# Two-layer diffusion trunk on one core: experts combined in token order, a last norm along the free axis, one-hot turns moved behind the first weight product

## The chip, the cores and the metric

One Trainium2 chip; the kernel runs on one of its cores. The time is device microseconds of one launch, the median of the runs; lower is better. The instruction streams of the core's engines are written out by hand and meet only at semaphores: TensorE (PE, with its weight loads PEld), VectorE (DVE), ScalarE (ACT), GpSimd (POOL) and SyncE (SP), which here issues the weight loads.

## What is computed

256 tokens of width 1024, with 256 context tokens, go through two layers. Only the end of the second layer concerns the change: a mixture of 8 experts, of which each token takes two, and the gated residual with its RMS norm.

```python
def moe_swiglu(h, router_w, w1, w3, w2):
    logits = (h @ router_w).astype(jnp.float32)
    top_val, top_idx = lax.top_k(logits, TOP_K)          # TOP_K = 2
    gates = jax.nn.softmax(top_val, axis=-1)
    dense_gate = jnp.sum(jax.nn.one_hot(top_idx, N_EXPERTS) * gates[..., None], axis=-2)
    out = jnp.zeros_like(h)
    for e in range(N_EXPERTS):                           # 8, inner width 3584
        out = out + dense_gate[..., e:e + 1] * swiglu(h, w1[e], w3[e], w2[e])
    return out
```

The layer ends with `x + gate * rmsnorm(moe_swiglu(...), g)`, where gate (from the conditioning) and g are vectors of width 1024. All arithmetic is held to fp32 accuracy: a matrix is split into a high and a low fp32r part, and a product is three products of those parts.

## The kernel before

**Weights.** SyncE loads all weights in units of 1 MB (128 x 2048 fp32) into a ring of six buffers, `raw_weights` (`RAW`), in one fixed order. An expert has 42 units (`NU`), numbered u0 to u41: for each of seven column blocks j two units of w1 (item "a"), two of w3 ("b") and two of w2 ("d"), in the order a0 b0, then a(j) b(j) d(j-1), and d6 last. ScalarE copies a unit to its high part (L1207), VectorE subtracts for the low part (L1523); there are three pairs of buffers for the parts (two are `split_high`/`split_low`, the third lies in `h_high`/`h_low`), so ScalarE waits until TensorE has used the pair. A raw buffer is free once its low part is made. The loads of the first expert take the buffers that the last earlier units leave: u0 the one of the last modulation weights, u1 the one of the router weights, which the router's last product (L1747) frees, and SyncE takes u2 to u5 behind u1.

**Start of the experts.** After the norm, TensorE multiplies by the router weights and transposes the normed tokens into token-major form (L1747, L1753). ScalarE and VectorE split these into `HTH` and `HTL` (L1169, L1431), VectorE finds the top two, the gates (`GATE`, tokens on partitions) and each token's slot in each expert, TensorE counting the positions (L1761 to L1765). VectorE makes one-hot matrices token by slot, `expert_onehot` (`MP`, L1467). `dispatch(0, r)` (L1798) gathers the first expert's tokens with them, in two halves of 16 products. Then TensorE turns all one-hots (L1785, ScalarE evacuates to `expert_onehot_t`, `MPT`, L1198), and multiplies them by the gates to get a gate for each slot (`slot_gates`, L1777). VectorE copies these (L1483), clears two banks and starts on the low parts of u0 and u1.

**One expert.** Up products write banks 0 to 3, down products accumulate in banks 4 and 5, slot by feature. The output of expert e-1 is handled inside expert e: `gated` (VectorE) scales banks 4 and 5 by the slot gate into `residual` (L1494), ScalarE makes the high part `ye_high` (L1190), VectorE the low part `ye_low` (L1501); `combine` (TensorE, L1870 and L1871, between a0 and b0) multiplies them by the turned one-hots, 16 products of 256 columns, which gives feature by token; `gather` (VectorE, L1510) adds four banks to `y` (`YACC`). For the first expert this handles a zero output, so there are nine combines. `dispatch(e + 1, r)` stands between d5 and d6 of expert e, on both sides of the last turn of the hidden state (L1840); it runs for the last expert too, with an empty one-hot.

**The end.** `YACC` is feature-major, so the last norm (n7) sums squares across partitions: ScalarE squares eight tiles (L351), TensorE sums (L365), ScalarE takes the root (L359), VectorE the reciprocal (L398), TensorE spreads it over partitions (L378), VectorE scales and adds to the residual (L449, L461), TensorE transposes the result (L1915), ScalarE evacuates (L1233) and SyncE stores two halves of 512 KB (L969). A branch for more than 128 tokens in an expert stands behind the experts; every engine reads its flag there.

## Time and profile before

| | |
|---|---|
| median of 3 runs | 2055.4 us (2053.35 to 2057.25) |
| the profiled execution, own time | 2057.55 us |
| its span, first to last instruction | 2055.7 us |
| busy: PE, DVE, ACT | 1928.8 (94%), 1296.7 (63%), 1088.1 (53%) us |
| granted TensorE clock, mean | 0.96 |
| HBM read | 471.25 MB, 230 GB/s over the span |

Times in the profile count from the span's first instruction. A timeline row gives start, duration and, in square brackets, the idle time of the engine before it and what ended it. Durations of matmuls are modelled and overlap; the difference between two starts is the pace. The granted clock is 1.00 at 2.4 GHz and 0.50 at 1.2 GHz.

### The profile page before, as it was taken

What the parts mean: (1) busy time and instruction counts of PE and PEld (TensorE: products, weight loads), DVE (VectorE), ACT (ScalarE), POOL (GpSimd) and SP (SyncE); (2) the same over time, 40 slices, a digit from 0 to 9 for tenths busy, and PEclk for the clock granted to TensorE, in tenths of its full rate; (3) what the DMA queues carried; (4) which work ended last, traced back from release to release, by engine and by line L of the source; (5) the groups of instructions that cost most, each with busy time, mean ns of one, the idle gap of its engine ahead of it and who ended that gap; (6) DMA issues with size and microseconds to landing.
All of it is one profiled execution on the core that took longest, in us unless ns stands there. A gap on an engine that the chain in (4) does not pass through costs nothing.

```text
span 2055.7 us, 24073 instructions
## 1 busy us (share of the span) xinstructions
PE 1928.8 (94%) x9978; PEld 1539.3 (75%) x9978; DVE 1296.7 (63%) x1252; ACT 1088.1 (53%) x1109; POOL 28.5 (1%) x44
## 2 busy tenths in 40 slices
PE   4998798999999989888899999999999999999996
PEld 2876476888878777457788787887888878888784
DVE  2344725323233462453788888888888888888885
ACT  3423435222232363354476676767767677676773
POOL 0000000000000000310000000000000000000000
PEclk9998899999999999897799999999999999999997
DMA  9453164533222270331699998999989999899990
GB/s 320 144 164 123 33 193 145 167 98 103 102 83 85 95 226 29 86 97 59 237 377 345 331 363 316 372 337 332 377 312 368 337 334 369 318 364 344 345 367 27
DMA packets 263942, 473.97 MB, mean 231 GB/s; under 512 B 17112, under 2 KB 116368, under 8 KB 263824
## 3 DMA queue, kind: packets, MB, share of 16 engines
q1 hardware_dynamic: 262928, 469.31, 65.2%
q0 software_dynamic: 896, 3.02, 0.5%
q8 instruction: 82, 1.34, 0.3%
q14 instruction: 36, 0.29, 0.0%
HBM read 471.25 MB, written 1.05 MB: 230 GB/s over the span
## 4 chain that ended last, share of the span: by engine, by line
PE 82%; DVE 9%; ACT 4%; DMA 2%; issue 2%; SPq 1%; POOL 0%; DVEq 0%; ACTq 0%
PE bank L508 24%; PE bank L510 23%; PE bank L509 23%; DVE split_low L1523 3%; PE bank L717 2%; PE bank L1798 2%; PE bank L571 2%; PE bank L1840 1%; DMA raw_weights<-in_w_mod 1%; PE bank L691 1%; DVE y L1510 1%; DVE h_low L1523 1%; PE bank L706 1%; SPq L907 1%; PE bank L365 1%
## 5 line engine op out<-in xcount | busy, mean ns | idle before, releaser
L1523 DVE TENSOR_TENSOR split_low<-raw_weights,split_high 128x2048 fp32r<-128x2048 f32 x224 | 512.5, 2288 | 53.3 <-ACT split_high L1207 51.5
L1207 ACT ACTIVATE split_high<-raw_weights 128x2048 fp32r<-128x2048 f32 x224 | 429.9, 1920 | 158.9 <-PE bank L510 158.9
L508 PE MATMUL bank<-h_high,split_high 128*128 128x512 f32 (+1 forms) x848 | 326.2, 385 | 21.7 <-DVE h_low L422 9.9
L492 DVE TENSOR_TENSOR split_low<-raw_weights,split_high 128x1024 fp32r<-128x1024 f32 x118 | 143.6, 1224 | 307.3 <-ACT split_high L487 307.3
L509 PE MATMUL bank<-h_low,split_high 128*128 128x512 f32 (+1 forms) x848 | 323.5, 381 | 0.0
L510 PE MATMUL bank<-h_high,split_low 128*128 128x512 f32 (+1 forms) x848 | 323.2, 381 | 0.0
L1523 DVE TENSOR_TENSOR h_low<-raw_weights,h_high 128x2048 fp32r<-128x2048 f32 x112 | 256.7, 2292 | 71.8 <-ACT h_high L1207 71.8
L508 PE MATMUL bank<-split_high,xe_high 128*128 128x512 f32 x672 | 270.7, 403 | 11.5 <-DVE split_low L1523 11.5
L509 PE MATMUL bank<-split_low,xe_high 128*128 128x512 f32 x672 | 265.9, 396 | 0.0
L510 PE MATMUL bank<-split_high,xe_low 128*128 128x512 f32 x672 | 265.9, 396 | 0.0
L1207 ACT ACTIVATE h_high<-raw_weights 128x2048 fp32r<-128x2048 f32 x112 | 214.9, 1919 | 53.2 <-PE bank L510 53.2
L487 ACT ACTIVATE split_high<-raw_weights 128x1024 fp32r<-128x1024 f32 x118 | 123.7, 1055 | 193.5 <-PE bank L510 189.3
L508 PEld LDWEIGHTS bank<-h_high,split_high 128*128 128x128 f32 x848 | 164.0, 193 | 54.5 <-issue 17.4
L510 PEld LDWEIGHTS bank<-h_high,split_low 128*128 128x128 f32 x848 | 163.7, 193 | 29.8
L509 PEld LDWEIGHTS bank<-h_low,split_high 128*128 128x128 f32 x848 | 164.1, 193 | 28.9
L508 PEld LDWEIGHTS bank<-split_high,xe_high 128*128 128x128 f32 x672 | 126.7, 189 | 42.5 <-issue 14.8
L510 PEld LDWEIGHTS bank<-split_high,xe_low 128*128 128x128 f32 x672 | 126.6, 188 | 30.3
L509 PEld LDWEIGHTS bank<-split_low,xe_high 128*128 128x128 f32 x672 | 126.9, 189 | 28.0
L508 PE MATMUL bank<-h_high,xe_high 128*128 128x512 f32 x224 | 89.1, 398 | 1.9 <-DVE h_low L1523 1.9
L508 PE MATMUL bank<-split_high,gt_high 128*128 128x512 f32 x224 | 89.1, 398 | 0.0
L508 PE MATMUL bank<-h_high,gt_high 128*128 128x512 f32 x224 | 88.5, 395 | 0.0
L509 PE MATMUL bank<-h_low,gt_high 128*128 128x512 f32 x224 | 88.5, 395 | 0.0
(246 smaller groups left out, 2630.4 us busy)
## 6 DMA issues: line engine op xcount, KB each, us to landing
raw_weights<-in_moe_w SPq DMA_DIRECT2D x336, 1024.0 KB, 6.7
raw_weights<-in_w_mod SPq DMA_DIRECT2D x48, 1024.0 KB, 6.0
raw_weights<-in_ffn_w SPq DMA_DIRECT2D x33, 1024.0 KB, 5.3
raw_weights<-in_ev_w_in SPq DMA_DIRECT2D x10, 1024.0 KB, 11.9
raw_weights<-in_od_w_in SPq DMA_DIRECT2D x8, 1024.0 KB, 7.1
raw_weights<-in_ev_w_out SPq DMA_DIRECT2D x4, 1024.0 KB, 8.9
raw_weights<-in_od_w_out SPq DMA_DIRECT2D x4, 1024.0 KB, 9.8
overlay<-in_rpb SPq DMA_DIRECT2D x32, 64.0 KB, 2.3
```

The costliest lines, as they stand in the source:

```text
L365: last = pe.matmul(n["sums"](j, t), ones[:, 0:32], n["sq"][:, t % 2, P * j:P * j + P], start=(t == 0 or n["single"]), stop=(t == n["nt"] - ...
L487: act.activation(half_of(s, j, SPH[:, s % NSPLIT, :]), half_of(s, j, raw_of(r)), ACT.Copy)\
L492: dve.tensor_tensor(half_of(s, j, SPL[:, s % NSPLIT, :]), half_of(s, j, raw_of(split_at[s])), half_of(s, j, SPH[:, s % NSPLIT, :]).bitcast ...
L508: pe.matmul(ps, wh, xh, start=first, stop=False)
L509: pe.matmul(ps, wh, xl, start=False, stop=False)
L510: return pe.matmul(ps, wl, xh, start=False, stop=last)
L571: last = pe.matmul(PS[bank][32 * j:32 * j + 32, 256 * (i % 2):256 * (i % 2) + 256], SC[:, 4 * h + j, :], wt[:, 4 * h + j, :], start=(h == ...
L691: last = pe.matmul(PS[2 * (i % 2) + m][:, :P * u["nk"]], u["q"][m], u["k"][m], start=True, stop=True)
L717: last = pe.matmul(pair_out(units, p)[0], u["v"][kt], PT[p % 2][:, kt, :], start=(kt == 0), stop=(kt == u["nk"] - 1))
L1207: act.activation(esplit(u)[0], RAW[:, u % NRAW, :], ACT.Copy).then_inc(S("e_high"), 1)
L1523: dve.tensor_tensor(lo, RAW[:, u % NRAW, :], hi.bitcast(F32), ALU.subtract)\
L1798: last = pe.matmul(PS[XBANK[r]][:, P * f:P * f + P], half[:, t, k:k + P], rhs, start=(n == 0), stop=(n == 3))
```

## The change

1. **Combine in token order.** `combine` takes the turned one-hots as the stationary operand and the high and low parts of the ungated output as the moving one: 8 products of 512 columns, token by feature. The gate is a scalar for each partition there, so `gather` becomes one multiply-add per bank with `GATE` as the scalar (for the first expert a plain multiplication). `gated`, `slot_gates`, the slot gates, the clearing of banks and of `YACC`, the ninth combine and the ninth dispatch go. ScalarE makes `ye_high` straight from banks 4 and 5.
2. **Last norm along the free axis.** `YACC` is token-major, so ScalarE squares four tiles with an accumulated row sum, and no cross-partition sum or spread is left. The product of conditioning gate and norm gain is needed as rows: VectorE builds eight diagonal tiles ahead of the router's result (`GDIAG`), TensorE sums them with a matrix of ones (two fp32 products of 512 columns) and ScalarE copies the result to `GROW`. TensorE transposes the residual without waiting for the norm; VectorE does the final multiply-add straight into the store buffer, and SyncE stores four pieces of 256 KB.
3. **Order at the start.** The high parts of u0 and u1 are made by ScalarE ahead of the copies of the token-major tokens; the low part of u0 by VectorE ahead of the router's result and that of u1 behind the first one-hot. The other one-hots come behind `xe_low`. TensorE turns the one-hots behind a0 instead of ahead of it, into banks 6, 7, 2 and 3. The table for Silu is loaded ahead of the experts, the one for Sqrt ahead of `moe_done`, VectorE's first instruction behind the branch.

The diff, cut to its core (counters of semaphores that only change their factor are left out):

```diff
+            for i in range(4):
+                t, c = i // 2, i % 2
+                sp.wait_ge(S("out_ready"), i + 1)
+                sp.dma_start(out[0, P * t:P * t + P, 512 * c:512 * c + 512], OUTT[:, i, :]).then_inc(S("stored"), 16)
+            sp.wait_ge(S("stored"), 64)
...
+            act.wait_ge(*unit_used(of["odo"][-1]))
+            for u in range(2):
+                act.wait_ge(S(f"eraw{u}"), 16)
+                act.activation(esplit(u)[0], RAW[:, u, :], ACT.Copy).then_inc(S("e_high"), 1)
...
+            for c in range(2):
+                act.wait_ge(S("grow_full"), c + 1)
+                act.activation(GROW[c], PS[6 + c][:, :].rearrange("p (a n) -> p a n", a=2), ACT.Copy)\
+                   .then_inc(S("grow"), 1)
+            act_table(act, ACT.Silu, 52)
...
+                    act.wait_ge(S("e_slots"), g0 + (e + 1) * NU + NSP_E)
                     for c in range(2):
-                        act.wait_ge(S("yg"), e * 2 + (2 * (NE + 1) * b + c + 1))
-                        act.activation(YEH[:, 512 * c:512 * c + 512], YG[:, 2 * c:2 * c + 2, :], ACT.Copy)\
+                        act.activation(YEH[:, 512 * c:512 * c + 512], PS[4 + c][:, :], ACT.Copy)\
                            .then_inc(S("ye_high"), 1)
...
+                            if b == 0 and e == 0 and u < 2:
+                                continue
...
-            act_squares(act, N["n7"])
-            act_root(act, N["n7"])
+            act_table(act, ACT.Sqrt, 53)
+            act.wait_ge(S("moe_done"), 1)
             for i in range(4):
-                act.wait_ge(S("out_full"), i + 1)
-                act.activation(OUTT[:, i // 2, 512 * (i % 2):512 * (i % 2) + 512], PS[i][:, :], ACT.Copy)\
-                   .then_inc(S("out_ready"), 1)
+                act.activation(SQUARED[i], YACC[i], ACT.Square, accum_out=SM[:, 12 + i:13 + i])\
+                   .then_inc(S("out_squares"), 1)
+            act.wait_ge(S("out_sums"), 1)
+            act.activation(SM[:, 18:20], SM[:, 16:18], ACT.Sqrt, bias=SM[:, 0:1], scale=1.0 / D).then_inc(S("out_root"), 1)
...
+            for k in range(KT):
+                last = dve.tensor_scalar(GDIAG[:, k // 2, k % 2, :], ident, VEC[:, 1, 3, k, 1:2], None, ALU.mult)
+            last.then_inc(S("grow_diag"), 1)
...
+            dve.wait_ge(S("e_high"), 1)
+            low_of(0)
...
+                onehot(0).then_inc(S("onehot_first"), 1)
                 if b == 0:
-
-                    dve.memset(GSL[:, 0:1], 0.0)
-                    dve.memset(MPT[:, 0, :].bitcast(F32), 0.0)
+                    dve.wait_ge(S("e_high"), 2)
+                    low_of(1)
                 xe_low(0, 0)
                 xe_low(0, 1)
-                if b == 0:
-                    link(dve, dve.memset(YACC, 0.0))
-                dve.wait_ge(S("gslot_full"), b + 1)
-                dve.tensor_copy(GSL[:, 1:NE + 1], PS[5][:, 32:40]).then_inc(S("gslot"), 1)
-                dve.wait_ge(S("gslot"), b + 1)
-                if b == 0:
+                for e in range(1, NE):
+                    last = onehot(e)
+                last.then_inc(S("onehot"), 1)
+
+                def ye_low(e):
+
                     for c in range(2):
-                        dve.memset(PS[4 + c][:, :], 0.0).then_inc(S("y_clear"), 1)
-                    dve.wait_ge(S("y_clear"), 2)
-
-                def gated(e):
-
-                    dve.wait_ge(S("e_slots"), e * NU + (g0 + NSP_E))
-                    for c in range(2):
-                        dve.tensor_scalar(YG[:, 2 * c:2 * c + 2, :],
-                                          PS[4 + c][:, :].rearrange("p (a n) -> p a n", a=2),
-                                          GSL[:, e:e + 1] if isinstance(e, int) else GSL[:, bass.ds(e, 1)], None,
-                                          ALU.mult).then_inc(S("yg"), 1)
-                    for c in range(2):
...
                     for r in range(4):
-                        dve.wait_ge(S("comb_full"), e * 4 + (4 * (NE + 1) * b + r + 1))
-                        acc = YACC[:, 2 * r:2 * r + 2, :]
...
+                        t, c = r % 2, r // 2
+                        dve.wait_ge(S("comb_full"), 4 * (NE * b + e) + r + 1)
...
+                        else:
+                            dve.scalar_tensor_tensor(acc, part, GATE[:, t, e:e + 1], acc, ALU.mult, ALU.add)\
+                               .then_inc(S("comb_done"), 1)
...
             dve.tensor_scalar(SM[:, 61:62], SM[:, 0:1], 1.0, None, ALU.mult).then_inc(S("moe_done"), 1)
-            dve_rstd(dve, N["n7"])
-            dve_residual(dve, N["n7"], 1, 1, 256)
+            dve.wait_ge(S("moe_done"), 1)
+            for i in range(4):
+                dve.tensor_tensor(OUTT[:, i, :].rearrange("p (a n) -> p a n", a=2), YACC[i], GROW[i % 2], ALU.mult)\
+                   .then_inc(S("out_scaled"), 1)
+            dve.wait_ge(S("out_squares"), 4)
+            sums = SM[:, 12:16].rearrange("p (t c) -> p t c", t=2)
+            dve.tensor_tensor(SM[:, 16:18], sums[:, :, 0], sums[:, :, 1], ALU.add).then_inc(S("out_sums"), 1)
+            dve.wait_ge(S("out_root"), 1)
+            link(dve, dve.reciprocal(SM[:, 20:22], SM[:, 18:20]))
+            dve.wait_ge(S("out_scaled"), 4)
+            for i in range(4):
+                dve.wait_ge(S("out_full"), i + 1)
+                dve.scalar_tensor_tensor(OUTT[:, i, :], OUTT[:, i, :], SM[:, 20 + i // 2:21 + i // 2],
+                                         PS[(0, 1, 4, 5)[i]][:, :], ALU.mult, ALU.add).then_inc(S("out_ready"), 1)
...
+            pe.wait_ge(S("grow_diag"), 1)
+            for c in range(2):
+                pe.matmul(PS[6 + c][:, :], ones, X[:, 4 + 2 * c:6 + 2 * c, 0:256], start=True, stop=True)\
+                  .then_inc(S("grow_full"), 1)
...
-                pe.wait_ge(S("onehot"), b + 1)
-                turn_onehots()
-                slot_gates()
-                pe.wait_ge(S("mpt_done"), 4 * b + 4)
-                if b == 0:
-                    pe.wait_ge(S("y_clear"), 2)
-                pe.wait_ge(S("gslot"), b + 1)
...
+                        if i == 0:
+                            pe.wait_ge(S("xe_low"), 2 * (NE * b + e) + q + 1)
...
-                        for f in range(2):
-                            k = P * (2 * r + f)
-                            o = PS[CBANK[r]][:, 256 * f:256 * f + 256]
...
-                            pe.matmul(o, YEH[:, k:k + P], rhs, start=True, stop=False)
-                            last = pe.matmul(o, YEL[:, k:k + P], rhs, start=False, stop=True)
-                        last.then_inc(S("comb_full"), 1)
+                        t, c = r % 2, r // 2
+                        pe.wait_ge(S("ye_low"), 2 * (NE * b + e) + c + 1)
+                        turned, y = MPT[:, e, P * t:P * t + P], slice(512 * c, 512 * c + 512)
+                        pe.matmul(PS[CBANK[r]][:, :], turned, YEH[:, y], start=True, stop=False)
+                        pe.matmul(PS[CBANK[r]][:, :], turned, YEL[:, y], start=False, stop=True)\
+                          .then_inc(S("comb_full"), 1)
...
-                            if j == 1:
-
-                                pe.wait_ge(S("comb_done"), e * 4 + (4 * (NE + 1) * b + 4))
+                            if j == 1 and e == 0:
+                                pe.wait_ge(S("mpt_done"), 4 * b + 4)
+                            elif j == 1:
+                                pe.wait_ge(S("comb_done"), 4 * (NE * b + e))
                             up(e, i, "a", j).then_inc(S("e_slots"), 1)
-                            if j == 0:
-                                combine(e)
+                            if j == 0 and e == 0:
+                                pe.wait_ge(S("onehot"), b + 1)
+                                turn_onehots()
+                            elif j == 0:
+                                combine(e - 1)
...
-                                dispatch(e + 1, 0)
+                                if e + 1 < NE:
+                                    dispatch(e + 1, 0)
                                 turn(e, JE - 1)
-                                dispatch(e + 1, 1)
+                                if e + 1 < NE:
+                                    dispatch(e + 1, 1)
...
-            pe_sums(pe, N["n7"])
-            pe_spread(pe, N["n7"])
-
             for i in range(4):
-                pe.wait_ge(S("n7_res"), 4 * (i % 2) + 4)
                 for k in range(4):
                     src = X[:, 4 * (i % 2) + k, CTX + P * (i // 2):CTX + P * (i // 2) + P]
-                    last = pe.transpose(PS[i][:, P * k:P * k + P], src, ident)
```

ScalarE's order from the normed tokens to the first expert; names in brackets are semaphores, `eraw1` is the landing of u1, `xe_full` the dispatch. Before:

```order
L345 ACTIVATE small<-small 128x1
L1169 ACTIVATE h_high<-bank 128x512 [waits htok_full] x4
L1172 ACTIVATE overlay<-overlay 128x2 [waits top_diff]
L1178 ACTIVATE xe_high<-bank 128x512 [waits xe_full] x2
L1198 ACTIVATE expert_onehot_t<-bank 128x512 [waits pt_full] x4
L1207 ACTIVATE split_high<-raw_weights 128x2048 [waits e_slots,eraw0]
L1207 ACTIVATE split_high<-raw_weights 128x2048 [waits e_slots,eraw1]
```

The changed kernel:

```order
L345 ACTIVATE small<-small 128x1
L1169 ACTIVATE split_high<-raw_weights 128x2048 [waits eraw0,bank_full]
L1169 ACTIVATE split_high<-raw_weights 128x2048 [waits eraw1]
L1174 ACTIVATE h_high<-bank 128x512 [waits htok_full] x4
L1177 ACTIVATE overlay<-overlay 128x2 [waits top_diff]
L1180 ACTIVATE residual<-bank 128x2x256 [waits grow_full] x2
L345 ACT_TABLE_LOAD
L345 ACTIVATE small<-small 128x1
L1188 ACTIVATE xe_high<-bank 128x512 [waits xe_full] x2
```

The two splits of weights moved from behind the turned one-hots to ahead of the four token copies. VectorE's order at a change of expert, before:

```order
L1523 TENSOR_TENSOR split_low<-raw_weights,split_high 128x2048 [waits e_high] x2
L1494 TENSOR_SCALAR residual<-bank,overlay 128x2x256 [waits e_slots]
L1494 TENSOR_SCALAR residual<-bank,overlay 128x2x256
L1501 TENSOR_TENSOR ye_low<-residual,ye_high 128x512 [waits ye_high] x2
L1523 TENSOR_TENSOR h_low<-raw_weights,h_high 128x2048 [waits e_high]
L1523 TENSOR_TENSOR split_low<-raw_weights,split_high 128x2048 [waits e_high]
L1510 TENSOR_TENSOR y<-bank,y 128x2x256 [waits comb_full] x4
L1523 TENSOR_TENSOR split_low<-raw_weights,split_high 128x2048 [waits e_high]
```

The changed kernel:

```order
L1424 TENSOR_TENSOR split_low<-raw_weights,split_high 128x2048 [waits e_high] x2
L1516 TENSOR_TENSOR ye_low<-bank,ye_high 128x512 [waits ye_high] x2
L1424 TENSOR_TENSOR h_low<-raw_weights,h_high 128x2048 [waits e_high]
L1424 TENSOR_TENSOR split_low<-raw_weights,split_high 128x2048 [waits e_high]
L1529 SCALAR_TENSOR_TENSOR y<-bank,overlay,y 128x2x256 [waits comb_full] x4
L1424 TENSOR_TENSOR split_low<-raw_weights,split_high 128x2048 [waits e_high]
```

The two gatings (L1494) are gone and nothing took their place; the adds became multiply-adds.

## Rows read from the trace of the kernel before

**Rows 1.** The expert phase, 1020 to 2020 us, by windows: length; busy PE PEld DVE ACT POOL; clock, DMA share, GB/s.
```profile
1020.00:2020.00 1000.00, 990.90 (x4546) 806.70 (x4545) 862.40 (x514) 700.48 (x469) 0.00 (x0) 1.00 0.94 342
```

**Rows 2.** Waits of 1020 to 2026 us: waiter, releaser, us in total, times, longest.
```profile
PE bank L508 <- DVE split_low L1523: 7.2, 7, 1.0
```

**Rows 3.** TensorE's timeline at one change of expert: start, duration, engine, line, operation.
```profile
1266.05 0.28 PE L1871 MATMUL bank<-expert_onehot_t,ye_low 128*128 128x256 f32 x1
1266.86 0.50 PE L508 MATMUL bank<-h_high,xe_high 128*128 128x512 f32 x1 [0.53 <-DVE h_low L1523]
...
1272.31 0.40 PE L510 MATMUL bank<-split_high,xe_low 128*128 128x512 f32 x1
1273.75 0.47 PE L508 MATMUL bank<-split_high,xe_high 128*128 128x512 f32 x1 [1.04 <-DVE split_low L1523]
```

**Rows 4.** VectorE's timeline at the same change of expert.
```profile
1260.60 1.41 DVE L1494 TENSOR_SCALAR residual<-bank,overlay 128x512 f32<-128x512 f32 x2
1262.05 1.35 DVE L1501 TENSOR_TENSOR ye_low<-residual,ye_high 128x512 fp32r<-128x512 f32 x2
...
1268.93 2.48 DVE L1510 TENSOR_TENSOR y<-bank,y 128x512 f32<-128x512 f32 x4
```

**Rows 5.** ScalarE's timeline at the same change of expert.
```profile
1261.38 1.29 ACT L1190 ACTIVATE ye_high<-residual 128x512 fp32r<-128x512 f32 x2 [3.02 <-DVE residual L1494]
1262.58 1.90 ACT L1207 ACTIVATE h_high<-raw_weights 128x2048 fp32r<-128x2048 f32 x1
```

**Rows 6.** TensorE's timeline from the first dispatch to the first weight product.
```profile
981.73 0.47 PE L1798 MATMUL bank<-expert_onehot,h_high 128*128 128x128 f32 x1 [2.75 <-DVE expert_onehot L1467]
...
988.62 3.62 PE L1785 MATMUL bank<-ident_r,expert_onehot 128*128 128x128 f32 x16
...
1002.90 0.77 PE L508 MATMUL bank<-split_high,xe_high 128*128 128x512 f32 x1 [3.95 <-DVE split_low L1523]
```

**Rows 7.** VectorE's timeline ahead of the first dispatch.
```profile
974.55 0.24 DVE L1411 COPY overlay<-bank 128x8 f32<-128x8 f32 x2 [6.04 <-PE bank L1747]
...
976.54 2.47 DVE L1431 TENSOR_TENSOR h_low<-bank,h_high 128x512 fp32r<-128x512 f32 x4
...
981.20 3.21 DVE L1467 TENSOR_SCALAR expert_onehot<-constants,overlay 128x128 fp32r<-128x128 f32 x16
```

**Rows 8.** SyncE's only expert load between 974.0 and 974.8 us, and its landing.
```profile
L920 SPq DMA_DIRECT2D raw_weights<-in_moe_w x1: 368/368/368, 974.5 to 974.5; - x1
...
DMA to landing us min/median/max: 5.1/5.1/5.1
```

**Rows 9.** The first 3 us of the weight products, by windows.
```profile
1003.00:1006.00 3.00, 3.00 (x7) 2.35 (x8) 3.00 (x3) 0.35 (x1) 0.00 (x0) 0.50 0.62 190
```

**Rows 10.** The costliest groups of 812 to 817 us: count, busy us, mean ns.
```profile
L1685 PE MATMUL bank<-raw_weights,overlay 128*128 128x512 f32 x8 | 3.7, 604 | 0.0
```

**Rows 11.** Timelines of VectorE and TensorE around the last expert's last down product.
```profile
2015.39 2.29 DVE L1523 TENSOR_TENSOR h_low<-raw_weights,h_high 128x2048 fp32r<-128x2048 f32 x1 [0.51 <-ACT h_high L1207]
...
2019.91 0.48 PE L508 MATMUL bank<-split_high,gt_high 128*128 128x512 f32 x1
```

**Rows 12.** VectorE's timeline from the last expert's end.
```profile
2025.79 1.41 DVE L1494 TENSOR_SCALAR residual<-bank,overlay 128x512 f32<-128x512 f32 x2 [4.36 <-PE bank L510]
...
2028.76 2.48 DVE L1510 TENSOR_TENSOR y<-bank,y 128x512 f32<-128x512 f32 x4 [0.17 <-PE bank L1871]
2033.88 0.15 DVE L1552 TENSOR_SCALAR small<-small 128x1 f32<-128x1 f32 x1 [2.63 <-issue]
```

**Rows 13.** ScalarE's timeline of the last norm and the output.
```profile
2038.58 1.28 ACT L359 ACT_TABLE_LOAD   x1
2039.88 0.36 ACT L359 ACTIVATE overlay<-bank,small 64x128 f32<-64x128 f32 x1
...
2052.09 0.60 ACT L1233 ACTIVATE overlay<-bank 128x512 f32<-128x512 f32 x1 [0.26 <-PE bank L1915]
```

**Rows 14.** ScalarE reading a row sum out of its accumulator (attention, earlier in the run).
```profile
881.30 0.19 ACT L733 ACTIVATION_READ_ACCUMULATOR y<-y,small 128x1 f32 x1
```

117 lines of the change are left out of this document (55 added, 62 removed).

## The prediction

> **What bounds the kernel now.** I read the windows first, then the waits, then the timelines of the three places that the change touches. The windows say that the expert phase is TensorE's: 990.9 of 1000 us busy at the full clock, while the DMA engines are 0.94 busy and VectorE 862 us [rows 1]. Nothing spread over that phase on another engine is worth anything; what counts is what TensorE executes there and where it stands still. The waits name VectorE's low parts, one kind of them once per change of expert, 7 times [rows 2]. Then there is a serial stretch on each side of the phase: from the router to the first weight product at 1002.90 [rows 6], and from the last combine to the end at 2055.7 [rows 12, 13]. In both TensorE's clock is low, but the engines wait for one another, so single latencies count.
>
> **1. Changes of expert.** TensorE starts the first product of b0 at 1266.86 where the pace of the combine (0.12) would have it at 1266.17: 0.69 lost. It starts a1 at 1273.75, and the pace of a 512-column product (0.23) would have given 1272.54: 1.21 lost [rows 3]. Together 1.90 us, at 7 changes 13.3 us. Both times a low part came late. VectorE had just done two gatings (1.41), two subtractions (1.35) and, later, four adds (2.48) [rows 4] beside its 2.29 per unit [rows 11]; and ScalarE had idled 3.02 us for the gated values, which put its high part of u2 off to 1262.58 [rows 5].
> In the changed kernel ScalarE makes `ye_high` as soon as the last down product is over (about 1258.9 on this clock) instead of at 1261.38, so its high part of u2 comes 2.4 us earlier, at 1260.2 to 1262.1. VectorE then does `ye_low` 1260.6 to 1262.0, u2 to 1264.4, u3 to 1266.6, the four multiply-adds to 1269.0 and u4 to 1271.2 (paces 2.2 and 0.62 from the rows). TensorE's combine is 8 products at 0.233 = 1.87 against 16 at 0.12 = 1.9: nothing gained or lost. It wants u2 at 1266.2 (1.8 to spare) and u4 at 1271.8 (0.6 to spare). I take both stalls as gone: **-13.3**. From below: a multiply-add out of PSUM is in no row; if it costs 0.1 more than the add, u4 still makes it; if it costs twice the add (2.5 more per change), u4 is 1.9 late and the gain is only the first stall, 0.7 x 7 = 4.8. From above: TensorE's other idle time is small, so 13.3 is nearly the end of what is there.
>
> **2. Start.** Removed from TensorE's way are the turns (3.62) and the slot gates behind them, with what followed: VectorE's copy, two clears and the low part of u0, the end of which is the wait of 3.95 before the first weight product [rows 6]. Now that product may follow the first dispatch at once. Dispatch ran from 981.73 to 988.62, so 1002.90 would become 988.7, **-14.2** [rows 6]. The turns come back behind a0 in the place of the first, empty combine, 16 products of 128 columns (half of 3.62, 1.8, at the full clock) against 1.9, even.
> But the change puts a wait on this path. ScalarE now makes the high part of u1 ahead of its copies of the tokens, and u1's load is issued at 974.5, when the router's product has freed the buffer, and lands 5.1 later, at 979.6 [rows 8]. Queued behind it on ScalarE: four copies, the exponential of the gates, the `GROW` copies, a table load. A unit's high part takes 1.90 [rows 5], so the copies start at 981.5 and the first is done at 982.1. VectorE's four token low parts, which began at 976.54 [rows 7], can begin at 982.1: **5.6 later**, and everything behind them (gates, positions, first one-hot, dispatch) moves by as much. First dispatch 987.3, first weight product 994.2: **-8.7** net. One more half microsecond comes back at a1, since u4 and u5 are no longer behind an empty gather; **-9.2** in all.
> At no cost, with their cover: the eight diagonals (0.20 each as the one-hots of [rows 7], 1.6) and u0's low part (2.3) lie in VectorE's 6.04 us of waiting for the router [rows 7]: u0's high part is made by about 972.2, its low part by 974.5, when the wait ends; without that cover they cost up to 3.9. The two `GROW` products: eight fp32 instructions of 512 columns took 3.7 at the full clock [rows 10], a product shows as two, so four at half the clock are 3.5 us. TensorE was idle 2.75 us before the dispatch [rows 6] and gets 5.6 more. The `GROW` copies (1.2) and the table load (1.3) fit between the exponential and the end of the first half of the dispatch, 3.4 us behind its start. Low part of u1: 2.3 under the dispatch.
> The clock: the first 3 us of weight products ran at half speed [rows 9]; I leave that as it is. If it rises at once, 1.6 more is gained; if it takes twice as long, 1.6 is lost.
>
> **3. Last expert.** Without the ninth dispatch d6 waits only for the last hidden state's turn, high and low part. VectorE is at u41 from 2015.39 until 2017.7 [rows 11], then makes `gt_low` (0.7): d6 can start at 2018.4 instead of 2019.91, **-1.5**. The 3.5 us of products removed are thus not all gained: a wait for VectorE takes their place.
>
> **4. End.** VectorE gates from 2025.79, right behind the last product, ScalarE and VectorE split, and the gather ends at 2031.24 [rows 12]. Without gating the combine starts 0.7 earlier, the gather ends at 2030.6. Then 2.63 us of flag and branch, kept, so `moe_done` is out at 2033.4. ScalarE: four squares of 512 columns (0.60 as the output copies in [rows 13]) with an accumulator read each (0.19, [rows 14]), at 0.78: until 2036.5. VectorE's four scalings (0.65 each) run beside them. Sum, root, reciprocal: 0.7, to 2037.2 (three tiny instructions with their hand-overs; the smallest one of VectorE's takes 0.15 [rows 12]). Four multiply-adds of 0.64: to 2039.8. From the last output copy's end, 2052.69, to the last instruction is 3.0 [rows 13], kept though the last piece is now half as large: end at 2042.8, **-12.9**. TensorE's 16 transposes of the residual can start behind the branch, about 2032; at the dispatch's pace (6.89 / 32 = 0.22 for 128 columns at half clock [rows 6]) they take 3.5, and even at twice that the last group is there when VectorE comes to it (2039.1).
> The table load for the root took 1.28 and the root started 1.30 after it [rows 13]; it is hidden now, and inside the 12.9. The Trainium skill (ScalarE: Activation LUTs, What ACT_TABLE_LOAD costs) puts a switch at about 2.66 us, with a drain behind the load. The trace does not show that drain here; by the page the end would gain 1.4 more.
>
> **Sum**: 13.3 + 9.2 + 1.5 + 12.9 = 36.9. Against the profiled execution: span 2055.7 becomes 2018.8, its own time 2057.55 becomes 2020.7. It was 2.15 above the median of the runs, so on the median 2055.4 I predict **2018.5**.
>
> **Rivals.**
> *VectorE still binds at the changes of expert.* For: 0.6 us to spare at u4 rests on four multiply-adds of unknown price. Against: the multiply-add reads as much as the add. It gives back 8.5 (13.3 - 4.8): 2027.0. Chance 0.14.
> *The clock rises earlier.* For: the `GROW` products are dense work shortly before the dispatch, and with a full clock dispatch takes half, 3.4 less, and the first 3 us of products 1.6 less: 2013.5. Against: 7 us of idling lie between, and dispatch and turns, 10 us without a pause, did not raise it [rows 6, 9]. Chance 0.07.
> *The loads become the bound, and the kernel gets slower.* Place: the raw ring through all eight experts. The DMA engines are 0.94 busy now [rows 1]. From 1002.90 [rows 6] to 2025.79 [rows 12] 336 units pass, one each 3.04 us; the change asks for one each 3.0. If a unit takes 3.11 us on the mean, 0.11 x 336 = 37 us eat the whole gain, and beyond that the kernel is slower; at 3.2 it would take 2018.5 + 67 = 2086. Against: the loads are the same ones, and in the expert phase no engine now waits for one (TensorE's own are for VectorE [rows 2]). Chance 0.02.
> *The change does not do what it says at the start*: five loads are issued together, and if they shared the engines evenly, u1 would land with the fifth, four units of 3.0 us later, and ScalarE would hold everything behind it. 9.2 gained becomes 2.8 lost: 2030.5. Against: the row gives this very load 5.1 us [rows 8]. Chance 0.03.
> The forecast itself: 0.74.
>
> **How the numbers follow.** What a measurement can tell from no change is about 0.2%, 4 us. Small errors in the forecast's own case (start by 3, end by 2, boundaries by 3) give 2014 to 2024. Taking in the first rival and half of the second the range is 2012.5 to 2028. Faster: 0.74 + 0.14 + 0.07 + 0.03 less a little for mistakes, 0.97; slower 0.02; same 0.01.
>
> **What would show it.** In the changed profile: no wait of TensorE for VectorE's low parts between 1000 and 2000, periods of 126 us instead of 127.9 (1022.9 / 8); ScalarE waiting for the DMA of u1 about 7 us ahead of the token copies; first dispatch near 987, first weight product near 994; d6's first product 2.4 us behind d5's end, waiting for VectorE; 9 to 10 us from `moe_done` to the end. The prediction is wrong if periods stay above 127, if ScalarE does not wait for u1 or the dispatch starts before 984, or if the tail waits for TensorE's transposes.

## The result, and the profile after

| | before | changed |
|---|---|---|
| median of the runs | 2056.32 us (4 runs, 2053.35 to 2058.32) | 2020.11 us (4 runs, 2018.66 to 2023.32) |
| profiled execution, own time / span | 2057.55 / 2055.7 | 2020.79 / 2018.6 |
| busy PE, DVE, ACT | 1928.8, 1296.7, 1088.1 us | 1908.7, 1278.3, 1083.9 us |

The ratio is 0.9821, 95% interval 0.9807 to 0.9834: 36.2 us faster, and 37.1 us by the two spans. The forecast was 2018.5 and 36.9.

**Expert phase.** The window that answers to [rows 1], and all the waits of TensorE from the first expert to the transposes of the last norm:

```profile
1001.00:2001.00 1000.00, 998.24 (x4525) 811.19 (x4524) 860.41 (x501) 708.67 (x477) 0.00 (x0) 1.00 0.95 345
```
```profile
PE bank L1936 <- issue: 2.9, 1, 2.9
PE bank L508 <- DVE gt_low L1534: 1.8, 1, 1.8
PE bank L1891 <- DVE ye_low L1516: 1.4, 1, 1.4
```

TensorE is busy 998.2 of 1000 us in place of 990.9. The seven waits for VectorE's low parts [rows 2] are gone; what is left is in the last expert and behind it. VectorE at one change of expert, which answers to [rows 4]:

```profile
1250.07 1.28 DVE L1516 TENSOR_TENSOR ye_low<-bank,ye_high 128x512 fp32r<-128x512 f32 x2
...
1255.70 2.72 DVE L1529 SCALAR_TENSOR_TENSOR y<-bank,overlay,y 128x512 f32<-128x512 f32 x4
```

Two gatings are gone, and the multiply-adds take 2.72 us for four where the adds took 2.48: the operation that no row of before priced costs 0.06 more apiece, not twice as much. The fifth unit's low part behind them ends 0.57 us before TensorE wants it.

**Start.** TensorE's timeline from the two new `GROW` products (first row) over the first dispatch and the first weight product to the start of a1, then ScalarE's and VectorE's around the wait that the change adds; they answer to [rows 6] and [rows 7]. The `GROW` products spread conditioning gate times norm gain over rows; some of the expectations below call them the product of tokens and gate.

```profile
974.25 3.62 PE L1794 MATMUL bank<-residual,constants 128*128 128x512 f32 x4
...
986.82 0.45 PE L1826 MATMUL bank<-expert_onehot,h_high 128*128 128x128 f32 x1 [7.59 <-DVE expert_onehot L1497]
...
993.68 0.73 PE L508 MATMUL bank<-split_high,xe_high 128*128 128x512 f32 x1
...
1009.14 0.47 PE L508 MATMUL bank<-split_high,xe_high 128*128 128x512 f32 x1
```
```profile
979.11 1.91 ACT L1169 ACTIVATE split_high<-raw_weights 128x2048 fp32r<-128x2048 f32 x1 [7.46 <-DMA raw_weights<-in_moe_w]
980.93 2.04 ACT L1174 ACTIVATE h_high<-bank 128x512 fp32r<-128x512 f32 x4
```
```profile
981.54 2.48 DVE L1460 TENSOR_TENSOR h_low<-bank,h_high 128x512 fp32r<-128x512 f32 x4 [5.49 <-ACT h_high L1174]
```

The first weight product comes 9.2 us earlier than before, and a1 follows without a gap. ScalarE did wait for u1's transfer, 7.46 us, VectorE 5.49 us for ScalarE behind it, and TensorE 7.59 us for VectorE. The granted clock over this stretch (columns as in [rows 1]):

```profile
976.00:978.00 2.00, 2.00 (x6) 0.97 (x4) 0.05 (x1) 0.00 (x0) 0.00 (x0) 0.50 1.01 390
979.00:981.00 2.00, 0.23 (x3) 0.14 (x2) 0.00 (x0) 1.89 (x2) 0.00 (x0) 1.00 1.05 393
983.00:986.00 3.00, 0.00 (x0) 0.00 (x0) 2.72 (x13) 2.52 (x5) 0.00 (x0) 0.50 1.05 387
990.00:998.00 8.00, 8.00 (x29) 7.09 (x29) 4.14 (x17) 2.99 (x3) 0.00 (x0) 0.50 0.61 223
999.00:1000.00 1.00, 1.00 (x6) 0.83 (x5) 1.00 (x1) 0.81 (x1) 0.00 (x0) 1.00 0.00 0
```

TensorE's clock went to its upper level (2.4 GHz) just as it ran out of work behind the `GROW` products, and was back at 1.2 GHz before the dispatch began.

**Last expert and end.** TensorE between the last turn and the last down product; then VectorE's tail, which answers to [rows 12]; then the stores:

```profile
1994.71 0.60 PE L1864 MATMUL bank<-constants,residual 128*128 128x128 f32 x4
1997.08 0.50 PE L508 MATMUL bank<-split_high,gt_high 128*128 128x512 f32 x1 [1.76 <-DVE gt_low L1534]
...
2002.52 0.39 PE L510 MATMUL bank<-h_high,gt_low 128*128 128x512 f32 x1
```
```profile
2005.09 2.73 DVE L1529 SCALAR_TENSOR_TENSOR y<-bank,overlay,y 128x512 f32<-128x512 f32 x4 [0.23 <-PE bank L1892]
2009.96 0.15 DVE L1574 TENSOR_SCALAR small<-small 128x1 f32<-128x1 f32 x1 [2.14 <-issue]
...
2013.46 2.72 DVE L1587 SCALAR_TENSOR_TENSOR overlay<-overlay,small,bank 128x512 f32<-128x512 f32 x4
```
```profile
2014.24 2.31 SPq L970 DMA_DIRECT2D out<-overlay  x4
```

From the start of the last down product to the end it is 16.08 us in place of 30.34.

**A table for all runs.** What lies ahead of the router's answer (VectorE's first copy of the logits, [rows 7]) is the same work for TensorE in all of these kernels, yet it ended anywhere from 968.4 to 976.6 us in their profiles. So times from there on are compared. One kernel repeated within 0.6 us; a further 1.7 us come from the clock, since the weight products behind the dispatches ran at 1.2 GHz for between 2.0 us (b1 and t1) and 5.3 us (changed, a0, l1) in profiles whose work up to there is the same. All are read from starts in the timelines of the profiled executions.

| kernel | answer | to first dispatch | to first weight product | to last down product | to the end | answer to end |
|---|---|---|---|---|---|---|
| before | 974.55 | 7.18 | 21.17 | 1022.46 | 30.34 | 1081.15 |
| changed | 973.97 | 12.85 | 6.86 | 1008.84 | 16.08 | 1044.63 |
| a0_changed, the same again | 974.70 | 12.79 | 6.86 | 1008.33 | 16.12 | 1044.10 |
| s1_u1_later | 968.58 | 7.27 | 6.86 | 1007.91 | 16.08 | 1038.12 |
| s2_turns_ahead | 972.16 | 12.79 | 14.68 | 1007.10 | 16.07 | 1050.64 |
| b1_vector_load | 976.08 | 12.78 | 6.86 | 1011.26 | 16.32 | 1047.22 |
| b2_gate_chain | 968.44 | 12.92 | 6.86 | 1021.21 | 16.07 | 1057.06 |
| t1_table_in_tail | 976.62 | 12.77 | 6.85 | 1006.91 | 17.35 | 1043.88 |
| l1_ninth_dispatch | 971.75 | 12.80 | 6.86 | 1009.95 | 16.14 | 1045.75 |
| t2_two_stores | 976.14 | 12.87 | 6.85 | 1008.50 | 16.84 | 1045.06 |
| w1_warm | 974.46 | 7.27 | 3.62 | 1005.94 | 16.31 | 1033.14 |
| c1_gates_later | 976.00 | 6.82 | 5.83 | 1007.10 | 16.35 | 1036.10 |
| c2_both | 974.45 | 6.80 | 4.20 | 1005.87 | 16.18 | 1033.05 |
| c3_three | 974.86 | 7.02 | 4.69 | 1007.83 | 16.20 | 1035.74 |

### The profile page after: what moved, and what is told of

It is laid out like the page before. It is cut to its first block, busy times and chain, and to the rows that moved or that the text cites. A ratio compares the mean times of both kernels' runs of the same rounds, so it can differ in the third digit from the quotient of the medians.

```text
span 2018.6 us, 23685 instructions
## 1 busy us (share of the span) xinstructions
PE 1908.7 (95%) x9802; PEld 1520.0 (75%) x9802; DVE 1278.3 (63%) x1219; ACT 1083.9 (54%) x1105; POOL 28.3 (1%) x44
## 4 chain that ended last, share of the span: by engine, by line
PE 88%; DVE 5%; ACT 3%; DMA 2%; SPq 1%; issue 1%; DVEq 0%; POOL 0%; ACTq 0%
PE bank L508 26%; PE bank L509 25%; PE bank L510 25%; PE bank L717 2%; PE bank L1826 2%; PE bank L571 1%; DMA raw_weights<-in_w_mod 1%; PE bank L691 1%; PE bank L1864 1%; PE bank L706 1%; SPq L907 1%; PE bank L378 1%; PE bank L365 1%; DVE small L778 1%; ACT split_high L487 1%
## 5 line engine op out<-in xcount | busy, mean ns | idle before, releaser
L510 PE MATMUL bank<-h_high,xe_low 128*128 128x512 f32 x224 | 88.5, 395 | 0.0
L509 PE MATMUL bank<-split_low,gt_high 128*128 128x512 f32 x224 | 88.5, 395 | 0.0
```

What stands on the lines that cost most here:

```text
L509: pe.matmul(ps, wh, xl, start=False, stop=False)
L510: return pe.matmul(ps, wl, xh, start=False, stop=last)
```

## The experiments

### What the stalls at the changes of expert came from

**b2_gate_chain** puts the old chain back, without the gate: VectorE multiplies twice behind the last down product, and ScalarE waits for it. What is computed stays the same.

```diff
 # ScalarE, ye_high, for c in range(2):
+                        if e < NE - 1:
+                            act.wait_ge(S("grow_diag"), 2 * ((NE - 1) * b + e) + c + 2)
 # VectorE, ye_low, first
+                    if e < NE - 1:
+                        dve.wait_ge(S("e_slots"), g0 + (e + 1) * NU + NSP_E)
+                        for c in range(2):
+                            dve.tensor_tensor(ov(11264 + 512 * c, 512), CON[:, 0:512], CON[:, 0:512], ALU.mult)\
+                               .then_inc(S("grow_diag"), 1)
```

> The same two multiplications, now behind the last product of the down projection, and ScalarE's copy of the high part waits for each, as it waited for the gate's multiplications in the kernel before; their results are not used, the sum in token order stays. Theory (the stalls of the kernel before came from this chain through the gate's multiplications and from nothing else): about 0.7 us to the first copy and 1.3 to the second come back into the chain, TensorE waits again at the seven changes, for ye_low and for the fifth unit, 1.6 to 1.9 us each: +11 to +13 us, 2031 to 2033.5. Rival (the gain came from the form of the sum or the adds, not from the chain): +5 us or less, as with the load alone.

Measured: 2031.24 us (ratio to before 0.9879, 0.9863 to 0.9894), 12.4 and 13.0 us more from the answer to the end than the two profiles of the changed kernel. Nearly all of it lies between the first weight product and the last down product. TensorE's timeline after the second expert, at the same two places as [rows 3], and its waits from 1004 to 1990 us:

```profile
1251.36 0.39 PE L1899 MATMUL bank<-ye_low,expert_onehot_t 128*128 128x512 f32 x1
1251.88 0.51 PE L508 MATMUL bank<-h_high,xe_high 128*128 128x512 f32 x1
...
1259.01 0.47 PE L508 MATMUL bank<-split_high,xe_high 128*128 128x512 f32 x1 [1.27 <-DVE split_low L1426]
```
```profile
PE bank L508 <- DVE split_low L1426: 8.9, 7, 1.3
PE bank L508 <- DVE h_low L1426: 0.2, 1, 0.2
```

The gaps between starts are 0.53 and 1.67 us, a pace of 0.23 taken off each: 0.3 + 1.44 = 1.74 per change, and the same at all seven to 0.05. That the chain through the gate stalls TensorE is shown; the form of the sum was kept, so it is not what removed the stalls. The size is not a copy of before's: there the two gaps made 1.56 to 1.60 at six changes and 1.90 at the one of [rows 3].

**b1_vector_load**: the same two multiplications, but nobody waits for them.

```diff
+                    if e < NE - 1:
+                        for c in range(2):
+                            dve.tensor_tensor(ov(11264 + 512 * c, 512), CON[:, 0:512], CON[:, 0:512], ALU.mult)
```

> Two idle multiplications of 128x512 are put into VectorE's order ahead of the low part of the expert's product at each of the seven changes of expert, about 1.3 us of work that nothing waits for, at a moment when VectorE has nothing ready. They come ahead of ye_low (1250.07 in the change after the second expert). Theory (VectorE's chain at a change has 0.57 us to spare at the fifth unit, and 2.0 at the third): the unit that binds comes 0.7 us late at each change, 7 x 0.7 = +5 us, 2025 (2023 to 2028). If instead VectorE works them off in the time in which it waits for the last down product (it has a gap there), the result is +0 to +1. Rival (VectorE has several us of slack at a change): no difference, within 0.2%.

Measured: 2023.33 us (0.9833, 0.9815 to 0.9851), 2.6 to 3.1 us more from the answer on. The same kind of wait is back, small:

```profile
PE bank L508 <- DVE split_low L1424: 2.4, 7, 0.6
```

The start of a1 is 0.70 or 0.71 us behind the product before it at six changes, and 0.99 after the second expert (a pace of 0.23 taken off, 0.47 and 0.76 lost), 3.6 in all. The short half-speed stretch of this profile hides about 1.7 of it. So VectorE's slack at a change is real and under a microsecond: of 1.2 us added, 0.47 to 0.76 came through. The estimate of 0.7 was too high for six of the changes, because there VectorE in the changed kernel also idled 0.21 us ahead of u2's low part, which took some of the load; after the second expert it did not, and there 0.76 were lost. Load alone explains somewhat over a quarter of b2; the rest is the wait.

### What the order at the start is worth

**s2_turns_ahead**: the turns of the one-hots ahead of the first weight product again.

```diff
                 dispatch(0, 1)
+                pe.wait_ge(S("onehot"), b + 1)
+                turn_onehots()
...
-                            if j == 0 and e == 0:
-                                pe.wait_ge(S("onehot"), b + 1)
-                                turn_onehots()
-                            elif j == 0:
+                            if j == 0 and e >= 1:
```

> The turns of the eight one-hot matrices are put back ahead of the first weight product, as the only difference from the changed kernel. Theory (the move takes a wait and the turns off the path): the first weight product waits for the last one-hot (998.0 in the changed kernel) and then for the turns at a half-speed clock, about 3.4 us, so it starts near 1001.5 instead of 993.68, 7.8 us later; the turns' 1.9 us behind the first group of products are saved: about +6 us, 2026 (2024.5 to 2027.5). Rival (the units that VectorE has yet to make bind the first expert anyway, so the order of the turns is worth nothing): +1 us or less.

Measured: 2026.07 us (0.9846, 0.9831 to 0.9861), 6.0 us more from the answer to the end (6.5 against the repeat): the first weight product 7.8 us later, 1.2 to 1.7 less behind it. TensorE:

```profile
996.16 3.67 PE L1815 MATMUL bank<-ident_r,expert_onehot 128*128 128x128 f32 x16 [4.15 <-DVE expert_onehot L1497]
999.63 0.73 PE L508 MATMUL bank<-split_high,xe_high 128*128 128x512 f32 x1
```

More than half of what the move saves is this wait of 4.15 us for the copies of the dispatches and 14 one-hots. The turns' own 3.5 us at 1.2 GHz come back behind a0 as 1.7. The first weight product came 14.3 us closer to the first dispatch with the change; this run accounts for 7.8 of it. The other 6.5 go with the slot gates and what followed them, which no run puts back; TensorE spent 6.9 us on their products in the kernel before:

```profile
992.03 6.93 PE L1777 MATMUL bank<-overlay,expert_onehot 128*128 128x1 f32 x32
```

**s1_u1_later** takes away the wait that the change added.

```diff
-            for u in range(2):
-                act.wait_ge(S(f"eraw{u}"), 16)
-                act.activation(esplit(u)[0], RAW[:, u, :], ACT.Copy).then_inc(S("e_high"), 1)
+            act.wait_ge(S("eraw0"), 16)
+            act.activation(esplit(0)[0], RAW[:, 0, :], ACT.Copy).then_inc(S("e_high"), 1)
...
             act_table(act, ACT.Silu, 52)
+            act.wait_ge(S("eraw1"), 16)
+            act.activation(esplit(1)[0], RAW[:, 1, :], ACT.Copy).then_inc(S("e_high"), 1)
```

> The high part of the second weight unit (u1) is made behind the copies of the product of tokens and gate, and no longer ahead of the token copies. The theory is that the changed kernel's start is bound by the wait for u1's transfer on ScalarE: 5.49 us in which VectorE waits for the token copies (981.54), and the first dispatch product at 986.82 behind it. Without it the token copies can start at about 975.4, the first dispatch product at about 981.3 and the first weight product at about 988 instead of 993.68, so 5.6 us less: about 2014.5 (2012.5 to 2016.5 with what the clock does). The rival is that something beside it (the router's answer and the positions, the turns of the one-hots, the units that follow) ends the start within a microsecond of it: then under 1 us less, 2019.2 to 2020.1.

Measured: 2014.98 us (0.979, 0.9773 to 0.9807), first dispatch 7.27 us behind the answer in place of 12.85: the 5.6 us, whole. From the answer to the end 6.0 to 6.5 less. So the changed kernel threw away 5.6 of the 14.3 us that it had gained at the start, and two lines in ScalarE's order bring them back.

### The clock of the start

**a0_changed** is the changed kernel unaltered, on the chip of the next three kernels. The kernel that they are made from, s1, ran on another chip, so differences from s1 of under a microsecond mean nothing.

> The changed kernel once more, unaltered, on the chip and in the rounds of the next three, so that differences of a few us can be read between them. From the router's answer to the end it took 1044.6 us in the profiled run (973.97 to 2018.6); what lies ahead of the answer moved by up to 7.7 us between the profiled runs of kernels that are identical there (968.43 to 976.08), which is the main part of their spread. Expected: 2018.5 to 2022, and 1044.6 within 1 us from the answer to the end.

Measured: 2019.40 us (0.9812, 0.9798 to 0.9826); 1044.10 us from the answer to the end, for 1044.63 in the first profile.

**w1_warm**: s1 with idle products in the gap ahead of the dispatches, into a bank that nobody reads.

```diff
+            for n in (512, 512, 256):
+                pe.matmul(PS[4][:, 0:n], ones, CON[:, 0:n], start=True, stop=True)
             pe.wait_ge(S("htok_low"), 4)
```

> The kernel with u1's high part later (first dispatch product 7.27 us behind the router's answer, then 6.86 us to the first weight product), with three idle 4-byte products of 128x512, 128x512 and 128x256 behind the positions, which fill the 2.4 us in which TensorE is idle ahead of the dispatches. In that kernel the granted clock was full from about 972 to 976 and fell to half as the dispatches began; it came back only near 986. Theory (the clock fell because TensorE was idle): it stays full, the dispatches take about half of their 6.86 us, and the weight products made at half speed (3.2 us of them) take half: up to -5 us from the answer to the end, unless the low part of u1 or the second expert_in half, which then come on the path, give some back: -2 to -5 us against the kernel it is made from (1038.1), so 1033 to 1036. Rival (the clock falls for another reason, or the copies and units behind the dispatches bind the first weight product): within 1 us of 1038.1.

Measured: 2008.14 us (0.9756, 0.9738 to 0.9774); 1033.14 from the answer to the end, 5.0 less than s1. TensorE, and the clock across the dispatches; then the same two for s1:

```profile
981.73 0.30 PE L1830 MATMUL bank<-expert_onehot,h_high 128*128 128x128 f32 x1
...
985.35 0.47 PE L508 MATMUL bank<-split_high,xe_high 128*128 128x512 f32 x1
```
```profile
980.00:982.00 2.00, 1.86 (x8) 0.87 (x6) 1.41 (x9) 1.99 (x3) 0.00 (x0) 1.00 1.06 393
982.00:984.00 2.00, 2.00 (x21) 2.00 (x19) 1.69 (x1) 0.54 (x2) 0.00 (x0) 1.00 1.05 387
```
```profile
975.85 0.45 PE L1827 MATMUL bank<-expert_onehot,h_high 128*128 128x128 f32 x1 [2.39 <-DVE expert_onehot L1498]
...
976.00:978.00 2.00, 2.00 (x10) 2.00 (x11) 1.57 (x1) 0.40 (x1) 0.00 (x0) 0.50 1.06 389
```

The clock stayed at 2.4 GHz, 3.24 us came off the dispatches and 2.0 off what follows. In s1 the same dispatches ran at 1.2 GHz behind 2.4 us of idling, and nothing but the idle products differs, so it was the idling. The Trainium skill (TensorE: Matmul & The Clock Gate, Part 1: The HAM clock gate) names the two levels and ties them to how busy TensorE has been; by that rule a filled gap keeps the upper one, and the trace agrees.

**c1_gates_later**: s1 with VectorE's gate arithmetic behind the first one-hots. **c2_both**: c1 and idle products of 512 and 256 columns.

```diff
-            dve.wait_ge(S("top_exp"), 1)
-            link(dve, dve.tensor_scalar(G1, EXP, 1.0, None, ALU.add))
...
                 onehot(0).then_inc(S("onehot_first"), 1)
+                if b == 0:
+                    dve.wait_ge(S("top_exp"), 1)
+                    link(dve, dve.tensor_scalar(G1, EXP, 1.0, None, ALU.add))
...
```

> The kernel with u1's high part later, and VectorE's arithmetic on the two gates (972.97 to 973.96 there, nothing reads them before the combine) moved from ahead of the positions to behind the first expert's one-hots. Theory (with u1's wait gone, VectorE's own chain bounds the first dispatch): the positions were ready at 973.47 on TensorE and VectorE took them up at 974.36, so about 0.9 us less: 1037.2 from the answer to the end in place of 1038.1. Rival: u1's low part and the one-hots come 1 us later behind it and nothing is gained.

> Both of the last two together, with idle products of 128x512 and 128x256 for the shorter gap. If each holds, the gains add: 1038.1 - 0.9 - (2 to 5) = 1032 to 1035 from the answer to the end, and about 2009 to 2012 by the runs' median, against about 2014.5 for the kernel with u1's high part later alone.

Measured: c1 2013.94 us (0.978, 0.9765 to 0.9795) and 1036.10 from the answer to the end, c2 2009.89 us (0.9768, 0.9753 to 0.9782) and 1033.05. In c1 the dispatch came only 0.45 us earlier (the other 1.6 are from a dispatch that began at 2.4 GHz, behind 1.53 us of idling, and fell to 1.2 GHz after 1.2 us, and from the clock behind it): VectorE then waited for TensorE's positions, which stand behind the `GROW` products.

```profile
981.32 0.17 DVE L1465 SCALAR_TENSOR_TENSOR overlay<-bank,overlay 128x16 f32<-128x16 f32 x1 [0.84 <-PE bank L1804]
```

In c2 nothing of it is left: with the gates ahead of it u1's low part begins at 982.41, and the first `xe_low` behind that at 984.62, against 982.31 and 984.52 in w1, whose answer came at the same moment. So c2's 1033.05 cannot be told from w1's 1033.14. The gains did not add; of the two predicted mechanisms the clock's was right and the gates' came at half its size.

**c3_three** changes three orders in c2: positions between the two `GROW` products, one idle product of 256 columns, and the first `xe_low` ahead of u1's low part (this last move is left out of the cut).

```diff
-            for c in range(2):
-                pe.matmul(PS[6 + c][:, :], ones, X[:, 4 + 2 * c:6 + 2 * c, 0:256], start=True, stop=True)\
-                  .then_inc(S("grow_full"), 1)
+            pe.matmul(PS[6][:, :], ones, X[:, 4:6, 0:256], start=True, stop=True).then_inc(S("grow_full"), 1)
...
-            for n in (512, 256):
+            pe.matmul(PS[7][:, :], ones, X[:, 6:8, 0:256], start=True, stop=True).then_inc(S("grow_full"), 1)
+            for n in (256,):
```

> The kernel with both changes of the start, with three orders changed: the positions' products ahead of the second product of tokens and gate (which then keeps TensorE busy in the gap, with one idle 128x256 product behind it), and the low part of the first dispatched half ahead of u1's low part. In the kernel with the gates later TensorE's positions bound the first dispatch (0.84 us of idle VectorE ahead of them), and with the idle products the first weight product waited behind u1's low part (984.52 for the first xe_low, whose high part ended at 984.34). Theory: the first dispatch product comes about 5.9 us behind the router's answer in place of 6.80, and the first weight product 3.6 behind it in place of 4.20: -1.5 us against 1033.05, so 1031.5 from the answer to the end and a median near 2008. Rivals: the clock does not rise (the idle filling is shorter), and 3 us of it is lost, 1034.5; or u1's low part is then late for the second half of a0, within 0.5 of 1033.

Measured: 2012.05 us (0.9763, 0.9741 to 0.9784); 1035.74 from the answer to the end, 2.7 us worse than c2: a miss, and neither of its rivals. TensorE and ScalarE:

```profile
979.14 2.05 PE L1804 MATMUL bank<-residual,constants 128*128 128x512 f32 x2
980.99 1.06 PE L1806 MATMUL bank<-constants 128*128 128x256 f32 x2
981.88 0.37 PE L1829 MATMUL bank<-expert_onehot,h_high 128*128 128x128 f32 x1
```
```profile
981.23 0.60 ACT L1179 ACTIVATE residual<-bank 128x512 f32<-128x512 f32 x1 [3.55 <-PE bank L1804]
981.85 1.28 ACT L345 ACT_TABLE_LOAD   x1
...
985.05 1.30 ACT L1189 ACTIVATE xe_high<-bank 128x512 fp32r<-128x512 f32 x2
```

The one-hots were ready near 980.7, but TensorE, now at 1.2 GHz until about 982, was still in the `GROW` product and the filler that I had sized for 2.4 GHz, so the first dispatch product began at 981.88. And on ScalarE the later copy pushed the table load, u1's high part and with them `xe_high` back to 985.05.

### The last expert and the end

**l1_ninth_dispatch** puts a ninth dispatch back behind the eighth expert (its result is not used; the helper `idle_dispatch`, 16 products for each half, is left out of the cut).

```diff
-                                if e + 1 < NE:
-                                    dispatch(e + 1, 0)
-                                turn(e, JE - 1)
-                                if e + 1 < NE:
-                                    dispatch(e + 1, 1)
+                                for r in range(2):
+                                    if e + 1 < NE:
+                                        dispatch(e + 1, r)
+                                    else:
+                                        idle_dispatch(r)
+                                    if r == 0:
+                                        turn(e, JE - 1)
```

> The changed kernel with the idle ninth dispatch back in the last expert, half of it ahead of the last turn and half behind it, on selectors of the eighth expert. It is read from the last up product to the last down product of the last expert. In the changed kernel TensorE waited there for the low part of the last turn (1.8 us idle) from the turn at 1994.71 to the down product at 1997.08. Theory: the half ahead of the turn (16 products, 1.7 us at full clock) delays the turn by that much, the half behind it hides in the wait: +1.7 us, less at most 0.2. Rival: both halves cost, +3.4; or both hide, 0.

Measured (one execution): from the product before the ninth dispatch to the next down product 4.16 us (1991.81 to 1995.97), against 2.60 in the changed kernel (1994.48 to 1997.08): +1.56. One half costs, the other hides in VectorE's work on the last turn. The kernel before had the same 4.16 there (2015.75 to 2019.91).

```profile
1991.81 0.39 PE L510 MATMUL bank<-split_high,gt_low 128*128 128x512 f32 x1
...
1995.97 0.45 PE L508 MATMUL bank<-split_high,gt_high 128*128 128x512 f32 x1
```

**t1_table_in_tail** leaves out the line `act_table(act, ACT.Sqrt, 53)`.

> The changed kernel without the early activation that loads the table of the square root. It is read by its tail: from the start of the last product of the down projection to the end it took 16.08, 16.12 and 16.07 us in three profiled runs. Theory (the early load at 2005.88 hides 1.28 us of table and 0.2 us of activation, and a load behind the last square would stand on the path): +1.3 us by the row, 17.4. The Trainium skill (ScalarE: Activation LUTs, section What ACT_TABLE_LOAD costs) would have it at +2.7 with the drain, 18.8. Rival (the load comes elsewhere, ahead of the squares, while ScalarE waits): no change, 16.1.

Measured (one execution): the tail is 17.35, +1.27 to the 16.08 (the tails of runs that leave the end alone lie between 16.07 and 16.35). ScalarE:

```profile
2013.48 1.28 ACT L1252 ACT_TABLE_LOAD   x1
2014.77 0.30 ACT L1252 ACTIVATE small<-small 128x2 f32<-128x2 f32 x1
```

The root starts 1.29 us after the load does. The Trainium skill (ScalarE: Activation LUTs, What ACT_TABLE_LOAD costs) adds a drain and comes to about 2.66 us; the measurement decides, and here a switch on the path costs the load alone.

**t2_two_stores**: one store of 512 KB per 128 tokens.

```diff
-            for i in range(4):
-                t, c = i // 2, i % 2
-                sp.wait_ge(S("out_ready"), i + 1)
-                sp.dma_start(out[0, P * t:P * t + P, 512 * c:512 * c + 512], OUTT[:, i, :]).then_inc(S("stored"), 16)
+            for t in range(2):
+                sp.wait_ge(S("out_ready"), 2 * t + 2)
+                sp.dma_start(out[0, P * t:P * t + P, :],
+                             OUTT[:, 2 * t:2 * t + 2, :].rearrange("p a n -> p (a n)")).then_inc(S("stored"), 16)
```

> The changed kernel with two stores of 512 KB, each when two blocks are ready, in place of four of 256 KB. In the changed kernel the first store is issued about 0.6 us behind the first block and the end comes 2.4 us behind the last multiply-add. Theory (the end is the last transfer's fixed cost and its bytes): the last transfer has twice the bytes, the tail of 16.1 us gets 0.5 to 0.7 longer. Rival (the transfers' fixed cost is all, and fewer issues are cheaper): 0 to -0.3.

Measured (one execution): the tail is 16.84, +0.76 to the 16.08, a little over the forecast. Four stores of half a row are the better choice here.

## Why the prediction was right

By the table, answer to end: +5.67 - 14.31 - 13.62 - 14.26 = -36.5, and the answer itself came 0.6 earlier by chance. The prediction had 36.9 in four terms.

1. **Changes of expert: -13.3 predicted, about -12.4 measured.** The mechanism holds (b2). The size was off: the 1.90 per change was read at one change, and its first stall, 0.69 [rows 3], is the largest; at the other six it is 0.37 to 0.40, the second stall 1.19 to 1.21 at all seven, together 11.4. A row of the same waits that [rows 2] leaves out would have shown it:

```profile
PE bank L508 <- DVE h_low L1523: 1.9, 7, 0.5
```

That is 0.27 of idling on the mean, not the 0.53 of [rows 3]. From one dispatch to the next the changed kernel takes 126.02 or 126.03 us six times (126 was forecast), the kernel before 127.74 to 128.12 seven times; over seven periods that is 12.4. The 1.0 beside the stalls is 0.15 a change, half of it from a combine of 1.83 us in place of 1.90, which the prediction had called even. The slack foreseen at u4, 0.6 us, is the 0.57 found, and b1 shows that it is little more than that.
2. **Start: -9.2 predicted.** The first weight product came at 993.68 for a predicted 994.2 (-8.6 from the answer on, for -8.7). The wait for u1 costs 5.6, shown alone (s1). Of the 14.3 gained, the move of the turns is shown alone (s2: 7.8 at the first weight product, 6.0 over the whole kernel); the rest, the slot gates and what followed them, is read from rows and not tested. The step "I leave that as it is" of the clock was off mildly: weight products ran at 1.2 GHz for 5.3 us and not 3.2, 1 us lost; b1 and t1, the same work up to there, had 2.0, so this term is partly chance. The cover for u0's low part held with nothing to spare: it ended at 973.97, the moment of the answer, and the answer came 0.90 us behind the start of the router's last product (0.97 before).
3. **Last expert: -1.5 predicted, -1.56 (l1).**
4. **End: -12.9 predicted, -14.26 measured.** Three terms were mis-sized, all too dear: the flag and branch took 2.14 us for 2.63, four squares came at the pace of the activation alone, 0.62 and not 0.78, since the accumulator reads overlap the next square, and the end lies 2.4 us behind the last multiply-add, not 3.0, with stores half as large (t2 has 0.76 of it back with the large ones). Against them the last multiply-adds, 0.68 for 0.64. The 1.4 us more are no drain behind the table load: t1 puts the load on the path and loses 1.27.

Of the signs that were named, only one was missed: from the flag (`moe_done`, 2010.11) to the end it is 8.5 us and not 9 to 10.

The forecast was thus 0.9 too high in the first term and 1.0 in the second, and 1.4 too low in the fourth: that the sum is 0.4 off is partly luck. Of the rivals, *VectorE still binds* fell with 0.57 us to spare. *The clock rises earlier* was half right in a way that I had not thought of: behind the new `GROW` products it did rise (in the kernel before it stood at 1.2 GHz from 958.4 to 1006.2), but 5 us too soon, and w1 shows that what the rival promised (5.0 us) is there to be had. *Loads* fell: DMA is 0.95 busy with TensorE at 998 of 1000. *u1 late with the fifth unit* fell: it landed at about 979.1.

The best version is w1, with c2 not to be told from it: 2008.14 us, 0.9944 of a0_changed's median on the same chip, and 11.0 us less from the answer to the end.

## What to carry to other kernels

When an element-wise step is folded into another, count the waits that go with it and not only its own time: here two multiplications of 0.6 us held up a chain of three engines and cost 1.74 us at each change of expert, while the same multiplications with nobody waiting cost about 0.5. When loads are moved forward in an engine's fixed order, look at what is queued behind their wait: 5.6 us were lost to a unit that TensorE did not touch before 998.9, 20 us after it had landed. And a gap of a few microseconds ahead of serial TensorE work may be worth filling with idle products, but only if they end before the gap does at the clock that they themselves run at.

## What the runs showed that I had not expected

The clock of TensorE can rise when its work is just over: in the changed kernel it was at 2.4 GHz from about 978.5 to 981.9, with TensorE idle from 979.2 on. Ahead of that it had stood at 1.2 GHz while TensorE worked without a pause at the router's products of 8 columns and transposes of 128, from 965 to 974. Then the length of the identical part ahead of the router's answer: 968.4 to 976.6 us over the profiled executions, which is most of the spread of every kernel's runs. It goes with the time that TensorE spent at 1.2 GHz on the way, summed here from the granted clock in windows of 8 us: 88 and 95 us in the two profiles with the earliest answers (968.4 and 968.6, b2 and s1), 101 to 118 in the other twelve (971.8 to 976.6), with a correlation of 0.9 over the fourteen. What makes the clock differ between executions of the same work stays open. And the half-speed stretch of the weight products was 2.0 us in b1 and 5.3 in the changed kernel behind the same gap and the same dispatches, so the clock's timing is not set by the program alone.
